# Two of the eight channel tiles of the first block's convolution on POOL, six on VectorE

## The reference

```python
def _conformer_conv(a_val, a_gt, w_dw, b_dw, ln_g, ln_b, w_pw, b_pw):
    u = a_val * jax.nn.sigmoid(a_gt)
    y = lax.conv_general_dilated(
        u, w_dw[:, None, :], window_strides=(1,), padding=[(CONV_KERNEL - 1, 0)],
        dimension_numbers=('NWC', 'WIO', 'NWC'), feature_group_count=CONV_WIDTH) + b_dw
    y = jax.nn.silu(_layernorm(y, ln_g, ln_b))
    return y @ w_pw + b_pw
```

## Time and profile before

| | |
|---|---|
| median of the runs | 2568.4 us |
| the profiled execution | 2565.47 us, span 2563.7 us |
| granted TensorE clock, mean | 0.991 |
| TensorE busy | 97% of the span |
| VectorE busy | 63% |
| ACT busy | 46% |
| POOL busy | 6% |

### The profile page before, as it was taken

How to read it: one execution, slowest core, us unless ns; L and a number is a source line. 1 busy time by engine, 2 the same in 40 slices (tenths; PEclk the granted TensorE clock), 3 DMA queues, 4 the chain that set the end, 5 groups by cost and what they waited for, 6 DMA issues and landing times.

```text
span 2563.7 us, 35901 instructions
## 1 busy us (share of the span) xinstructions
PE 2486.2 (97%) x14366; PEld 2175.2 (85%) x14366; DVE 1622.7 (63%) x1941; ACT 1176.6 (46%) x1371; POOL 151.1 (6%) x136
## 2 busy tenths in 40 slices
PE   6999999999889999999999999999999999999998
PEld 6888998898778788988888888888888888888886
DVE  4799755545674776486565545445677557755764
ACT  5433754444464554542345444334655334433333
POOL 0000000000200100000000000000022001210220
PEclk9999999999999999999999999999999999999999
DMA  7565436554424555554026555535455555655553
GB/s 236 165 197 189 142 131 229 150 165 133 144 83 159 157 185 172 170 164 132 1 82 214 187 180 192 164 132 184 160 182 196 192 183 183 196 187 185 186 174 138
DMA packets 341284, 422.91 MB, mean 165 GB/s; under 512 B 14491, under 2 KB 267178, under 8 KB 340394
## 3 DMA queue, kind: packets, MB, share of 16 engines
q1 hardware_dynamic: 338620, 411.66, 49.1%
q0 software_dynamic: 2160, 8.40, 1.0%
q10 hardware_dynamic: 382, 1.11, 0.1%
HBM read 419.05 MB, written 2.10 MB: 164 GB/s over the span
## 4 chain that ended last, share of the span: by engine, by line
PE 94%; DVE 4%; ACT 2%; issue 0%; DMA 0%; ACTq 0%; DVEq 0%
PE ps L678 29%; PE ps L679 15%; PE ps L723 9%; PE ps L725 9%; PE ps L724 9%; PE ps L681 4%; PE ps L682 4%; PE ps L683 4%; PE ps L944 3%; PE ps L754 1%; DVE w_lo L1844 1%; PE ps L912 1%; PE ps L885 1%; PE ps L1141 1%; PE ps L1132 1%; PE ps L901 0%
## 5 line engine op out<-in xcount | busy, mean ns | idle before, releaser
L678 PE MATMUL ps<-h_cat,w_hi 128*128 128x512 f32 x3200 | 1137.0, 400 | 8.2 <-DVE qo L1877 8.0
L679 PE MATMUL ps<-h_cat,w_lo 128*128 128x256 f32 x3200 | 897.7, 281 | 0.0
L1844 DVE TENSOR_TENSOR w_lo<-ring,w_hi 128x2048 fp32r<-128x2048 f32 (+2 forms) x282 | 592.3, 2102 | 278.6 <-ACT w_hi L1221 275.6
L678 PEld LDWEIGHTS ps<-h_cat,w_hi 128*128 128x128 f32 x3200 | 602.2, 188 | 159.1 <-DVE w_lo L1844 6.1
L679 PEld LDWEIGHTS ps<-h_cat,w_lo 128*128 128x128 f32 x3200 | 605.5, 189 | 2.1 <-issue 1.9
L1221 ACT ACTIVATE w_hi<-ring 128x2048 fp32r<-128x2048 f32 (+2 forms) x282 | 495.8, 1759 | 98.9 <-PE ps L725 84.5
L1840 DVE TENSOR_TENSOR w_lo<-ring,w_hi 128x2048 fp32r<-128x2048 f32 (+1 forms) x136 | 303.1, 2232 | 232.0 <-ACT w_hi L1218 231.9
L1218 ACT ACTIVATE w_hi<-ring 128x2048 fp32r<-128x2048 f32 (+1 forms) x136 | 252.7, 1862 | 285.4 <-PE ps L725 263.4
L723 PE MATMUL ps<-w_hi,h_cat 128*128 128x512 f32 x704 | 275.9, 392 | 4.7 <-DVE h_cat L2013 3.0
L725 PE MATMUL ps<-w_hi,h_cat 128*128 128x512 f32 x704 | 274.7, 390 | 0.0
L724 PE MATMUL ps<-w_lo,h_cat 128*128 128x512 f32 x704 | 274.7, 390 | 0.0
(11 more groups left out here) (380 smaller groups left out, 2460.0 us busy)
## 6 DMA issues: line engine op xcount, KB each, us to landing
ring<-in_w_ffn_up SPq DMA_DIRECT2D x44, 2048.0 KB, 8.0
ring<-in_even_w_in SPq DMA_DIRECT2D x28, 2048.0 KB, 8.1
ring<-in_w_mix_in SPq DMA_DIRECT2D x28, 2048.0 KB, 8.3
ring<-in_w_ffn_down SPq DMA_DIRECT2D x16, 2048.0 KB, 8.0
ring<-in_odd_w_in SPq DMA_DIRECT2D x11, 2048.0 KB, 8.3
ring<-in_even_w_out SPq DMA_DIRECT2D x8, 2048.0 KB, 8.1
ring<-in_odd_w_out SPq DMA_DIRECT2D x8, 2048.0 KB, 8.1
ring<-in_w_mix_out SPq DMA_DIRECT2D x8, 2048.0 KB, 8.1
```

The costliest lines, as they stand in the source:

```text
L678: mm(o[:, 0:2 * T], whi[slot][:, k, :], flat(cat[:, k]), start=first, stop=False)
L679: ins = mm(o[:, T:2 * T], wlo[slot][:, k, :], cat[:, k, 0, :], start=False, stop=end)
L1844: tt(wlo[slot][:, 0:g.kt, 0:m], chunk(c % RING, g)[:, :, u0:u0 + m], whi[slot][:, 0:g.kt, 0:m].bitcast(F32), ALU.subtract).then_inc(sem["l ...
```

## The change

POOL takes the first pair of tiles. For each of the 31 taps it makes one product of 2 x 256 elements per partition into a new buffer `tapped` (the weight is broadcast along the tokens), and one addition onto `conv`; each of these 62 instructions waits for the one before it by the semaphore `pool_tap`. The first waits until the first two tiles of `u` are there. VectorE makes the taps of the other three pairs, 186 in place of 248, and its schedule per unit becomes 6 taps from the seventh unit of `e_val` on, 7 in `e_v`, and 6, 6, 6, 4 in the first four units of `e_bgate`. The drains of `e_bgate` and the sum over channels also wait for `pool_tap` to reach 62. `tapped` lies over scratch space that nothing uses in this stretch.

```diff
+    tapped = place("tapped", [P, 2, T], off=XSQ)
...
+        pool.wait_ge(sem["params_ready"], 2)
+        pool.wait_ge(sem["posted"], S["e_val"].s0 + 2)
+        for tap in range(TAPS):
+            w = prm[:, COL["dw"] + tap * CT:COL["dw"] + tap * CT + 2].unsqueeze(2).to_broadcast([P, 2, T])
+            if tap:
+                pool.wait_ge(sem["pool_tap"], 2 * tap)
+            pool.tensor_tensor(tapped[:], u[:, 0:2, tap:tap + T], w, ALU.mult).then_inc(sem["pool_tap"], 1)
+            pool.wait_ge(sem["pool_tap"], 2 * tap + 1)
+            before = conv[:, 0:2, :] if tap else prm[:, COL["b_dw"]:COL["b_dw"] + 2].unsqueeze(2).to_broadcast([P, 2, T])
+            pool.tensor_tensor(conv[:, 0:2, :], tapped[:], before, ALU.add).then_inc(sem["pool_tap"], 1)
         pool.wait_ge(sem["acc_ready"], S["o_gate1"].n0 + 8)
...
-                    pe.wait_ge(sem["conv_tap"], TAPS * CT)
+                    pe.wait_ge(sem["conv_tap"], TAPS * (CT - 2))
+                    pe.wait_ge(sem["pool_tap"], 2 * TAPS)
...
-                act.wait_ge(sem["conv_tap"], 2 * TAPS * (j // 2 + 1))
+                act.wait_ge(sem["pool_tap"], 2 * TAPS)
+                if j >= 2:
+                    act.wait_ge(sem["conv_tap"], 2 * TAPS * (j // 2))
...
-                for n in range(first + at * per_unit, min(first + (at + 1) * per_unit, CT * TAPS)) if at >= 0 else ():
-                    two, tap = n // (2 * TAPS), n % (2 * TAPS) // 2
+                for n in range(first + at * per_unit, min(first + (at + 1) * per_unit, (CT - 2) * TAPS)) if at >= 0 else ():
+                    two, tap = n // (2 * TAPS) + 1, n % (2 * TAPS) // 2
...
-        seg("e_val", conv_taps(0, 7, 4), unrolled=True)
-        seg("e_k", conv_taps(28, 7), unrolled=True)
-        seg("e_q", conv_taps(84, 7), unrolled=True)
-        e_v_taps = conv_taps(140, 8)
+        seg("e_val", conv_taps(0, 6, 6), unrolled=True)
+        seg("e_k", conv_taps(12, 6), unrolled=True)
+        seg("e_q", conv_taps(60, 6), unrolled=True)
+        e_v_taps = conv_taps(108, 7)
...
-            taps = conv_taps(204, 11)
+            taps = conv_taps(164, 6)
```

More of the change, by code:

```diff
@@ L381, in build @@
              "ht_hi", "ht_ready", "tiles_read", "agate_read", "hhi_ready", "h_ready", "x_normed", "gain1_loaded", "gain_out_loaded",
-             "conv_tap", "conv_mean", "conv_centred", "conv_sq", "conv_var", "conv_std", "conv_normed", "conv_silu",
+             "conv_tap", "pool_tap", "conv_mean", "conv_centred", "conv_sq", "conv_var", "conv_std", "conv_normed", "conv_silu",
              "scores_ready", "masked", "max_ready", "exp_done", "p_ready", "pt_turned", "pt_ready",
```

## The result

The changed kernel takes 2608.1 us (median of 4 runs, 2606.34 to 2609.73) against 2568.3 us before (median of 4 runs). The ratio is 1.0159, with a 95% interval from 1.0147 to 1.0171: 40 us slower. The forecast was 2622 us.

A forecast was written before the change was run, and what follows sets the result against it. TensorE, busy 97% of the span, was taken to bound the kernel. Slowed steps of 103.8 us against 42.9, less 4.8 and 1.9, lose 54 us: 2568.4 + 54 = 2622 us, range 2588 to 2660.

The forecast's parts named there:

- POOL is slow by itself: Rival, chance 0.05: without exclusion, POOL's long instructions end at 240 us, hidden, or at 302 us, making ACT wait: 2610 us.
- VectorE keeps the port: Rival, chance 0.17: POOL makes about one instruction per unit, the rest run alone while ACT waits at `e_bgate`: 2613 us.
- TensorE does not wait before: From 60 to 460 us TensorE never waits, so taking 62 taps, 25 us, off VectorE gains nothing.
- VectorE and POOL exclude each other: VectorE instructions with two SBUF inputs and POOL instructions reading SBUF keep each other out, 1.15 and 0.99 us in the trace.
- They take turns: Main case, chance 0.65: VectorE and POOL alternate one instruction each during the convolution; 2622 us, own range 2594 to 2655.
- The sum: Slowed steps in `e_val` and `e_k` last 103.8 us against TensorE's 42.9; less 4.8 and 1.9 us, 54 us lost.
- the price of a turn: VectorE time lost to each POOL instruction in a slowed step, taken as 1.1 us.
- four free instructions of POOL: Before the first taps VectorE has about 3.5 us free, so some 4 POOL instructions cost nothing and 58 are left.
- the slack of 4.8 us: Time between the addition of line 1877 ending at 93.15 and TensorE's turn at 97.93, subtracted from the loss.
- The clock: TensorE's lower level, some 11 us a unit, stays covered by VectorE's steps but for the end: a few us.
- The waits of TensorE: TensorE idle 7 to 8.5 us per unit on line 1877, from the seventh unit of `e_val` to mid `e_k`.
- POOL done before `e_bgate`: POOL done at some 198 us, before the first drain of `e_bgate` at 260.30, so that wait costs nothing.

The follow-up runs named there:

- run 1: Changed kernel without POOL's 62 products and sums, two tiles cleared once, VectorE's schedule and waits kept: 2567.5 us, ratio 0.9999 to the kernel before.
- run 4: Changed kernel with 62 POOL memsets, which write as much and read nothing, in place of products and sums: 2567.3 us, ratio 0.9997 to the kernel before.
- run 5: Changed kernel with 62 one-input POOL copies in place of products and sums: 2574.8 us, ratio 1.0034 to the kernel before.
- run 6: Changed kernel with all of POOL's work, VectorE keeping only the first tap of each tile: 2568.6 us, ratio 1.0006 to the kernel before.
- runs 2 and 3: Changed kernel with half of POOL's instructions: 31 products alone, 2580.2 us, ratio 1.0047; 31 sums alone, 2585.7 us, ratio 1.0068 to the kernel before.

## Why the prediction was right, point by point

- **The time alone does not show it.** 2608 us is nearer to the 2610 and 2613 us of two rivals than to the forecast's 2622. The profile decides: "POOL is slow by itself" wanted POOL at work until 302 us, or 240 without a loss, and "VectorE keeps the port" wanted it at work into `e_v`; it is done at 185 us, and no drain of `e_bgate` waited for it.
- **TensorE does not wait before, so the relief is worth nothing.** Right: run 1 gives VectorE the relief alone and changes nothing.
- **VectorE and POOL exclude each other.** Right, and shown from both sides: without reads by POOL no loss (run 4), with one read a small one (run 5), with room on VectorE no loss (run 6).
- **They take turns.** Right. The open question, who wins when VectorE's next instruction is ready, is answered by the eight POOL instructions in a step with eight candidates. VectorE does not keep the port.
- **The sum.** The forecast was 54 us, the stretch cost 41.0 us. The term that was mis-sized is the price of a turn: 1.1 us, where the traces show 0.86 to 0.88. 58 turns x 0.23 us = 13 us, the size of the whole difference. With 12.3 and 11.1 us a step, the same working gives 5 x 12.3 + 2.6 x 11.1 - 42.9 - 6.7 = 41 us. Two things made the price too high. I took one kind for both: a product starts 1.17 us before the next instruction (111.52 to 112.69), a sum 1.43 us (112.69 to 114.12), of which a tap takes 0.40; that leaves 0.90 us on average. (It comes to 0.86 because POOL's instruction behind the split, 108.22 to 111.44, runs partly beside line 1891 and costs nothing there.) And I added the 0.10 us by which POOL had started first, though with turns that start lies beside VectorE's own instruction.
- **Two small errors that cancel.** I counted four free instructions of POOL; the trace has six before line 1896 at 98.82 us, so 56 turns cost and not 58 (1.7 us too much). And I took off 1.9 us because VectorE would come early to the first of the slowed steps. It came early to the split, at 94.53, but then waited 1.41 us for ACT, and the slowed steps begin at 98.36 (1.9 us too little). That the sum with the measured steps meets 41 so closely is partly luck. Counted from the trace, eight steps from 98.36 to 188.63 last 90.3 us, where TensorE needs 8 x 5.65 = 45.2 us; less the slack of 4.8 us that is 40.3 us. The 0.7 us to 41.0 are in the next point.

```profile
98.36 0.42 DVE L1891 TENSOR_TENSOR stage<-stage,ps 128x256 f32<-128x256 f32 x1 [1.41 <-ACT stage L1247]
...
188.63 0.41 DVE L1891 TENSOR_TENSOR ke<-ke,ps 128x256 f32<-128x256 f32 x1
```

- **The clock.** The mean in 88 to 200 us is 0.86. TensorE's waits on line 1891 sum to 28.8 us while 41.0 are lost; the other 12 us are units that TensorE ran at its lower level inside steps that VectorE made 11 to 12 us long. They are a loss of their own only at the end, as forecast. VectorE is busy without a pause from step to step, so a slower unit inside a long step delays nothing. The last unit that waited starts at 181.79 and ends at 189.78, 8.0 us in place of 5.65; the granted clock is 0.50 from 181 to 185 us. VectorE's addition for the next unit was done at 189.04, so the lower level cost 0.7 us of the 41.0, where I had allowed a few.

```profile
181.79 0.77 PE L689 MATMUL ps<-h_cat,w_hi 128*128 128x512 f32 x1 [5.08 <-DVE ke L1891]
...
189.78 0.38 ACT L1251 ACTIVATE ke<-ps 128x256 f32<-128x256 f32 x1 [10.86 <-PE ps L690]
```

- **The waits of TensorE.** Forecast 7 to 8.5 us per unit, measured 6.4 us at most. With steps of 12.3 and 11.1 us and units of 5.65 us, 6.6 and 5.5 us are left to wait; units at the lower level shorten that.
- **POOL done before `e_bgate`.** Right, at 185 us against 198 forecast.

## What to carry to other kernels

Before moving work from VectorE to POOL, look at what VectorE runs at that time. If its instructions read two SBUF tensors, as the taps here, POOL's reading instructions are paid for in VectorE's time, here more than twice what they saved, and the move pays only where VectorE has idle time of that size and something waits for it. A trace that has POOL at work anywhere shows it: pairs of rows in which one engine's instruction is longer by what the other's had left.

## What the runs showed that I had not expected

The alternation in the change is exact: while taps of 0.40 us follow each other with no pause, POOL still gets a turn after each, eight in a step with eight candidates. It broke only where POOL came late (runs 2 and 3). A VectorE instruction with only one SBUF tensor, the `tensor_scalar` of the first taps, is kept out too (1.444 us against 0.410), even by memsets (0.692 us, run 4), while the addition with its other input in PSUM is not (0.40 to 0.43 us in the runs above).
